# A hybrid decoder step: the last memory update reordered, and four sequences' cached values side by side on TensorE

## What is computed

```
z = rmsnorm(x) @ w_in                       # q, k, v for two groups of 8 heads, an output gate, gates
o_a = dilated sliding-window attention      # heads of group A, three (window, dilation) patterns
h_b = mLSTM matrix memory                   # heads of group B: C, n, m are carried along
x  += concat(rmsnorm(o_a), sigmoid(gate) * rmsnorm(h_b)) @ w_out
x  += conv_glu(rmsnorm(x));  x += sigmoid(rmsnorm(x) @ w_g) * (p @ w_p)
```

## Time and profile before

| | us |
|---|---|
| median of 3 runs | 3385.48 (3385.16 to 3386.03) |
| the profiled execution's own time | 3385.48 |
| its span | 3383.7 |
| TensorE busy | 3175.6 (94%) |
| VectorE busy | 1972.8 (58%) |
| mean granted TensorE clock | 0.97 of full |

### The profile page before, as it was taken

The page is one execution under the profiler, slowest core; times in us unless marked ns, Lnnn a source line. Parts: engine busy times, 40 slices in busy tenths (PEclk is TensorE's granted clock), DMA queues, the critical chain, the costliest instruction groups (busy, mean ns, idle before and its releaser), DMA issues. The chain is left out here.

```text
span 3383.7 us, 49227 instructions
## 1 busy us (share of the span) xinstructions
PE 3175.6 (94%) x19573; PEld 2881.5 (85%) x19573; DVE 1972.8 (58%) x4354; ACT 980.3 (29%) x2029; POOL 624.9 (18%) x564
## 2 busy tenths in 40 slices
PE   7899999888999999998998998996999999999989
PEld 6777677578999999998987776773989999999988
DVE  5666454666555555558556654557575555555573
ACT  4333334533111111114233333444321112111131
POOL 2001111202231122211211110122032122212210
PEclk8999999889999999999999999997999999999999
DMA  5111122621111111110221111327111111111101
GB/s 158 52 47 45 51 71 68 186 79 51 50 51 51 38 51 50 50 38 19 90 59 51 45 45 43 78 77 208 47 63 48 41 44 57 39 50 38 54 19 68
DMA packets 209869, 208.77 MB, mean 62 GB/s; under 512 B 36676, under 2 KB 183044, under 8 KB 207536
## 3 DMA queue, kind: packets, MB, share of 16 engines
q1 hardware_dynamic: 209640, 205.62, 20.4%
HBM read 173.96 MB, written 31.61 MB: 61 GB/s over the span
## 5 line engine op out<-in xcount | busy, mean ns | idle before, releaser
L791 POOL TENSOR_TENSOR wlo<-raw,whi 128x512 fp32r<-128x512 f32 (+3 forms) x488 | 592.5, 1249 | 2214.3 <-ACT whi L1332 2214.3
L832 PE MATMUL ps<-hi,wlo 128*128 128x344 f32 x2880 | 933.4, 324 | 27.0 <-DVE wb L2219 15.5
L833 PE MATMUL ps<-lo,whi 128*128 128x344 f32 x2880 | 926.7, 322 | 0.0
L834 PE MATMUL ps<-hi,whi 128*128 128x344 f32 x2880 | 926.3, 322 | 0.0
L832 PEld LDWEIGHTS ps<-hi,wlo 128*128 128x128 f32 x2880 | 547.4, 190 | 29.9 <-DVE wb L2219 16.1
L833 PEld LDWEIGHTS ps<-lo,whi 128*128 128x128 f32 x2880 | 547.2, 190 | 0.6
L834 PEld LDWEIGHTS ps<-hi,whi 128*128 128x128 f32 x2880 | 547.2, 190 | 0.0
L832 PE MATMUL ps<-whi,lo 128*128 128x512 f32 (+5 forms) x1152 | 448.0, 389 | 19.4 <-ACT zt L1387 18.6
L834 PE MATMUL ps<-whi,hi 128*128 128x512 f32 (+5 forms) x1152 | 425.3, 369 | 0.0
L833 PE MATMUL ps<-wlo,hi 128*128 128x512 f32 (+5 forms) x1152 | 423.6, 368 | 0.0
L2231 DVE TENSOR_TENSOR X<-X,ps 128x344 f32<-128x344 f32 x528 | 268.4, 512 | 196.1 <-PE ps L834 195.6
(11 more groups left out here) (293 smaller groups left out, 3962.6 us busy)
## 6 DMA issues: line engine op xcount, KB each, us to landing
raw<-in_w_up SPq DMA_DIRECT2D x44, 1024.0 KB, 5.1
raw<-in_w_in SPq DMA_DIRECT2D x112, 256.0 KB, 4.6
raw<-in_w_down SPq DMA_DIRECT2D x22, 1024.0 KB, 4.9
kvb<-in_cache_win_k SPq DMA_DIRECT2D x48, 256.0 KB, 3.2
cache<-in_cache_win_v SPq DMA_DIRECT2D x42, 256.0 KB, 5.5
x_scratch<-X SPq DMA_DIRECT2D x8, 1032.0 KB, 5.0
X<-x_scratch SPq DMA_DIRECT2D x4, 2064.0 KB, 14.2
raw<-in_w_out SPq DMA_DIRECT2D x8, 1024.0 KB, 6.4
```

The lines of the kernel that those rows point to most:

```text
L791: pool.tensor_tensor(out=wlo[:, s, r], in0=raw[:, s, r], in1=whi[:, s, r].bitcast(F32), op=ALU.subtract).then_inc(w_split, 1)
L832: nc.tensor.matmul(out, a_lo, b_hi, start=first, stop=False)
L833: nc.tensor.matmul(out, a_hi, b_lo, start=False, stop=False)
L834: return nc.tensor.matmul(out, a_hi, b_hi, start=False, stop=last)
```

## The change

- **The values of four sequences side by side.** `pZ` holds 32 columns for each pattern and sequence instead of a staircase of 64. The 24 products become two groups of 12 (at c = 3 and at c = 5), each of four sequences: sequence g of a group writes PSUM rows 32g to 32g + 31, with a stationary block of 128 x 32, in bank 6 or 7. So the sum that follows runs on 128 rows x 2 banks, and the new token's own part, which was added in place, goes through DRAM: a store (`Sd[2]`), a wait for it, and four loads into `so`. The result goes back by four stores instead of one.
- **Order of VectorE's list.** The root of the attention output's squares moves from the head of the last pair to c = 2, behind `memory_gates`, which comes there from c = 3; `memory_keys`, `memory_output`, `memory_update` come one step earlier each (c = 3, 4, 5). At c = 6 the squares of tiles 0 to 4, their root and `normalise(0)`, `normalise(1)` are done; tiles 5 to 7 follow later.
- **TensorE** turns y tile 0 ahead of the turn of the last memory; **ScalarE** does the output gate behind the exponentials of the decay, and scales and rounds each w_out block in two steps.
- **SyncE.** w_out blocks 2 and 3 come behind `zb` and the slices 0 to 9; `state_C` behind the thirteen small loads; half of x behind the gate's round trip; the own part's store, a wait for it and its four loads come next; then one wait for 12 products, and the slices 19 to 23.

```diff
@@ sp, pair 6 and last pair
-                    load_pair(p + 3)
+                    if p < 2 * PAIRS - 2:
+                        load_pair(p + 3)
...
                 sp.wait_ge(*at(gemm_done, GEMM_OUT))
-                sp.dma_start(lof[:, 0:2048], A["state_C"][l].rearrange("b h (x v) k -> (b h x) (v k)", x=2)).then_inc(cst_in, 16)
...
                     sp.dma_start(zb[:, j, :], Zd[j].rearrange("b (h d) -> (b h) d", d=HD)).then_inc(zb_in, 16)
+                for i in range(10):
+                    load_values(i)
+                load_pair(2 * PAIRS + 1)
...
                 sp.dma_start(mz[:, 2 * HD:2 * HD + 32], Zd[5].rearrange("b (r d) -> (b r) d", d=32)).then_inc(mz_in, 16)
-                for i in range(19):
+                sp.dma_start(lof[:, 0:2048], A["state_C"][l].rearrange("b h (x v) k -> (b h x) (v k)", x=2)).then_inc(cst_in, 16)
+                for i in range(10, 19):
                     load_values(i)
...
                     load_y(t)
-                sp.dma_start(X[:, 0:4, :], Xd[:, 0:4, :]).then_inc(x_back[0], 16)
                 sp.wait_ge(*at(o_exp, PAIRS))
                 sp.dma_start(Zd[6, :, WA - P:WA], zt[0:NB, last % 2, NT, OG:ZW]).then_inc(z_stored[last % 2], 16)
                 sp.wait_ge(*at(z_stored[1], stored_value(last)))
                 sp.dma_start(mz[:, 2 * HD + 32:3 * HD], Zd[6].rearrange("b (r d) -> (b r) d", d=32)).then_inc(mo_in, 16)
+                sp.dma_start(X[:, 0:4, :], Xd[:, 0:4, :]).then_inc(x_back[0], 16)
+                sp.wait_ge(*at(own_done, 1))
+                sp.dma_start(Sd[2].rearrange("b (h d) -> (b h) d", d=HD), sv[:, 0, :]).then_inc(own_stored, 16)
+                sp.wait_ge(*at(own_stored, 16))
+                sp.wait_ge(*at(pz_set, 2))
+                for g in range(4):
+                    sp.dma_start(so[32 * g:32 * g + NH, :, :], Sd[2][g:NB:4, :].rearrange("j (h d) -> h j d", h=NH)).then_inc(so_in, 16)
+                sp.wait_ge(*at(v_used, 12))
                 for i in range(19, 24):
-                    sp.wait_ge(*at(v_used, i - 18))
                     load_values(i)
@@ pe, sample_values
-                        for i in range(5 * c - 15, min(3 * NB, 5 * c - 10)) if c >= 3 else ():
-                            b, r = divmod(i, 3)
-                            a = r * WA + b * HD
-                            pe.wait_ge(*at(v_in[i // 6], 96))
-                            nc.tensor.matmul(ps[0:HD, 6, :], pZ[:, a:a + HD], value_place(i), start=(i == 0), stop=(i == 23)).then_inc(v_used, 1)
+                        if c not in (3, 5):
+                            return
+                        half = (c - 3) // 2
+                        for x in (0, 1):
+                            pe.wait_ge(*at(v_in[2 * half + x], 96))
+                        for r in range(3):
+                            for g in range(4):
+                                b = 4 * half + g
+                                a = (r * NB + b) * 32
+                                nc.tensor.matmul(ps[32 * g:32 * g + 32, 6 + half, :], pZ[:, a:a + 32], value_place(3 * b + r),
+                                                 start=(r == 0), stop=(r == 2)).then_inc(v_used, 1)
...
+                    if q + 1 == PAIRS:
+                        turn_y(0)
                     pe.wait_ge(*at(c_upd, 9 * (q + 1)))
@@ act, last pair
-                    if q + 1 == PAIRS:
-                        output_gates(p)
...
                         do(nc.scalar.activation(sm, sm, ACT.Exp, scale=SCALE, bias=small[:, 10:11], accum_out=small[:, 11:12]), sp_exp)
+                        output_gates(p)
...
-                for t in range(3):
-                    y_high(t)
+                y_high(0)
+                output_squares(PAIRS - 1, NT - 1)
+                y_high(1)
+                y_high(2)
@@ dve, last pair
                         elif c == 2:
                             sample_turned()
+                            memory_gates()
+                            rsqrt(yrs[:, 0:NT], yt2[:, 0:NT], ssq[:, 0:NT], WA, ya_rs)
                         elif c == 3:
-                            memory_gates()
+                            memory_keys()
                         elif c == 4:
-                            memory_keys()
+                            memory_output()
                         elif c == 5:
-                            memory_output()
+                            memory_update()
                         elif c == 6:
-                            memory_update()
+                            y_root(0, 5)
+                            normalise(0)
+                            normalise(1)
...
+                normalise(2)
+                dve.wait_ge(*at(cs_out, 16))
                 for t in range(3):
-                    normalise(t + 2)
...
                     y_low(t)
+                y_root(5, NT)
+                normalise(3)
+                normalise(4)
+                sample_out()
                 sample_sum()
```

More of the change, by code:

```diff
@@ L1055, in gate_columns, with turn_y @@
                     mm.then_inc(gc_ready, 1)
+                def turn_y(t):
+                    m = rows(t)
+                    pe.wait_ge(*at(yn_done, t + 1))
+                    if t < NT:
+                        pe.wait_ge(*at(ya_done, t + 1))
+                    if t >= 2:
+                        n = min(t - 1, NT - 1) + t // NT
+                        pe.wait_ge(*at(yh_done, 2 * n))
+                        pe.wait_ge(*at(yl_done, 2 * n))
+                    for k in range(KT):
+                        mm = nc.tensor.transpose(ps[:, y_bank(t) + k // 4, (k % 4) * m:(k % 4 + 1) * m],
+                                                 y_stage(t)[0:m, k * P:(k + 1) * P], ident[0:m, 0:m])
+                    mm.then_inc(yt_ready, 1)
                 for q in range(PAIRS):
@@ L1187, in turn_embedding @@
                     mm.then_inc(pt_ready, 1)
-                for t in range(3):
+                for t in (1, 2):
                     turn_y(t)
@@ L1949, in memory_update, with y_root, normalise @@
                     do(v.scalar_tensor_tensor(out=Cs, in0=Cs, scalar=iw_, in1=Ct, op0=ALU.mult, op1=ALU.add), mem_done)
+                def y_root(first, end):
+                    dve.wait_ge(*at(ysq_done, NT * (PAIRS - 1) + end))
+                    own = slice(NT + 1 + first, NT + 1 + end)
+                    do(v.tensor_reduce(out=ssq[:, own], in_=ysq[:, :, first:end].rearrange("p q t -> p t q"), axis=AX.X, op=ALU.add))
+                    rsqrt(yrs[:, own], yt2[:, own], ssq[:, own], WA, None)
+                def normalise(t):
+                    m = rows(t)
+                    y = y_stage(t)
+                    rs = yrs[0:m, NT + 1 + t:NT + 2 + t]
+                    if t < NT:
+                        dve.wait_ge(*at(yb_done, NT * (PAIRS - 1) + t + 1))
+                        dve.wait_ge(*at(yst_in[t % 4], 16 * (t // 4 + 1)))
+                        do(v.tensor_scalar(y[:, WA:D - P], y[:, WA:D - P], rs, None, ALU.mult), wait=False)
+                        do(v.tensor_scalar(y[:, D - P:D], yb[:, t, :], rs, None, ALU.mult), yn_done, wait=False)
+                    else:
+                        do(v.tensor_scalar(y[0:m, 0:WA], y[0:m, 0:WA], yrs[0:m, NT:NT + 1], None, ALU.mult), wait=False)
+                        do(v.tensor_scalar(y[0:m, WA:D], y[0:m, WA:D], rs, None, ALU.mult), yn_done, wait=False)
                 for q in range(PAIRS):
@@ L1972, in _ @@
                     evac_k(p)
-                    if last:
-                        rsqrt(yrs[:, 0:NT], yt2[:, 0:NT], ssq[:, 0:NT], WA, ya_rs)
                     if q:
@@ L1992, in queries_scaled @@
                         do(v.tensor_copy(cwb[:, :], iwb[:, P - 1:SEQ:P]))
-                        do(v.tensor_tensor(out=iwb, in0=qT[:, :], in1=iwb, op=ALU.mult), ib_used)
+                        do(v.tensor_tensor(out=iwb, in0=qT[:, :], in1=iwb, op=ALU.mult))
                         if q > 1:
```

98 lines of the change are left out of this document (37 added, 61 removed).

## The result

The kernel after takes 3408.14 us (median, 3403.99 to 3410.15), the kernel before beside it on the same chip 3385.76 us (3385.16 to 3386.11): a ratio of 1.0066, 95% interval 1.0054 to 1.0078. The profiled execution took 3409.46 us and its span is 3407.6 us, 23.9 us more than before.

A forecast was written before the change was run, and what follows sets the result against it. TensorE's dense weight products bound the kernel, so each microsecond the first w_out product moves counts; late value slices move it 7.3 us per layer, + 14.6 us for two: 3385.5 + 14.6 = 3400 us, own range 3391 to 3408 (chance 0.52).

The forecast's parts named there:

- The sign and the mechanism: Slower: in each layer's last pair late value slices (last at 685.5) hold the second group 14.5 us; w_out 7.3 us later.
- one constant: From the second group's start to the first w_out product, through updates, VectorE's steps and turns: 28.3 us.
- The group: TensorE's 12 value products, side by side in column blocks and begun at half clock, take 5.3 us.
- the rival, 13.1 us: Column blocks don't run side by side: a group takes 13.1 us, 7.8 more per layer, kernel 3416; chance 0.10.
- The slow stretch: DMA behind the n_p stores moves 61 GB/s from 635 to 643, now falling on the first value slices.
- The own part's store: SyncE's store of the own part waits behind half of x (2.11 MB, 5.8 us) and lands at 678.3.
- the rival in which it does: The own part's store passes half of x: 5.8 us fall away, kernel 3388; chance 0.22 together with a short hole.
- The step that was too small: SyncE's issues (13 x 0.64 + 19 x 0.50 + 3 us) are done by 657; DMA engines are through at about 669.
- Layer 1: Same order and nearly the same times as layer 0: 7.3 us later there too, + 14.6 us for both layers.
- The rival "no wait": Last slice is there when TensorE comes at 671.0; w_out at 699.3, 7.2 us earlier, kernel 3371; chance 0.16.

The follow-up runs named there:

- x behind: The kernel after, with half of x loaded behind value slices 19 to 23: 3394.45 us, ratio to the kernel before 1.0030.
- own store early: The kernel after, with the own value's store issued right behind the last small load, x left in place: 3400.62 us, ratio to the kernel before 1.0049.
- n_p late: The kernel after, with the third memory pair's n_p stores issued behind slices 19 to 23: 3403.79 us, ratio to the kernel before 1.0057.
- w_out early: The kernel after, with w_out's blocks 2 and 3 loaded in their old place: 3397.07 us, ratio to the kernel before 1.0034.
- all three: The kernel after, with w_out in its old place, n_p stores and half of x behind slices 19 to 23: 3381.10 us, ratio to the kernel before 0.9991.
- the old queue: All the change's work, with SyncE's list in the order of the kernel before plus the own store and its return: 3389.52 us, ratio 1.0016.
- the old work with the early queue: The kernel before, with SyncE's list of the 3368 run (slices early, n_p stored late): 3378.27 us, ratio to the kernel before 0.9981.
- the last slices early: The kernel after, n_p late, w_out early, slices 0 to 11 first, 19 to 23 ahead of every return trip: 3368.14 us, ratio 0.9951; the fastest run.
- in the early queue: The 3368 run with the third pair's n_p stores put back ahead of the sample loads: 3372.84 us, ratio to the kernel before 0.9968.

## Why the prediction was right, and the step that was too small

*The sign and the mechanism held.* The last slices set the end of the stretch: TensorE idles 13.07 us ahead of the second group (14.5 predicted), released by the value cache's DMA. That the two waits agree so well is luck in part, for both of its ends came later than predicted: the slices were there at 689.4 and not 685.5, and TensorE came to them at 676.4 and not 671.0, since the first group had waited for its own slices until 665.2 and not 660.5. The median, 3408.14, lies at the very end of the forecast's own range, 3391 to 3408. The kernels with the new work whose second group waits for slices give one constant from its start to w_out in layer 0: 28.5 us after, and 28.1, 28.8, 28.6, 29.0, 28.6 and 28.5 in the runs with x behind, own store early, n_p late, w_out early, all three and the old queue (28.3 predicted).

*The group.* 5.25 us at half clock (5.3 predicted). The price of the rival, 13.1 us, was measured as well: 13.12. At half clock the old product's 0.90 us would be 1.80 (an estimate); 5.25 us for twelve are 0.44 each, a quarter. The Trainium skill, TensorEngine Tiling (Array Packing), "Theoretical Speedup", gives a speedup of up to 4 for 32 columns; the trace agrees.

*The slow stretch* lay where predicted, 633 to 642 at 41 GB/s, full rate from 642.

*The own part's store* needed 7.9 us behind half of x (7.8 predicted, 670.5 to 678.3). It did not pass it; the rival in which it does is out. The Trainium skill, DMA: Bandwidth & Descriptors, "Queues, rings and completion order", says that each DMA engine takes its work in ring order and that a later transfer may complete first. The runs agree with the first half: where the own store stands right behind half of x it takes 7.0 to 7.9 us, and in the old order the gate's store behind half of x takes over 12. No run here shows the second half.

*The step that was too small* is "Issuing isn't the limit: ... done by 657". It took each issue at its undisturbed price, and it priced the thirteen small loads at 1.1 us of transfer, although they hold SyncE for 8.3 us in which nothing large is issued. The slices' ten took 9.81 us and not 5, w_out's 2.08, the first small load 3.62, so that state_C went out at 657.3 and slice 18 at 662.7, y's three by 664.9; the DMA engines stood nearly still from 654 to 658 in between. Against 362 GB/s, the 105 and 12 GB/s of those 4 us lack some 3.4 us of transfer (an estimate), nearly all of what is missing here: the gate's store is back at 673.3 instead of 669.5, and this 3.8 us runs through unchanged. Last slice at 689.4 and not 685.5, w_out at 717.95 and not 713.8.

Two edits move the gate store: w_out's load out of the way by 7.6 us (1.9 of them because the stretch starts earlier), the n_p stores out of the way by 6.4 (658.62; 2.1 of them the same). They don't tell issuing from transfer: the 5.7 us left for w_out are what the prediction gave its transfer, 5.8. But the run with w_out early has the dry stretch without the blocked issue, so the small loads one by one are enough for it.

*Layer 1* was taken as equal, + 7.3; w_out's shift there, beyond that of layer 0, is + 13.0. But the stretch itself loses hardly more or less than in layer 0. Counted from the y store at its head, w_out comes 11.5 us later than before in layer 0 and 11.1 in layer 1. The other 1.9 us arise between the two stretches: layer 1's already begins 13.3 us late.

```profile
2291.93 0.38 SPq L670 DMA_DIRECT2D y_scratch<-yb  x1
```

```profile
2305.21 0.39 SPq L676 DMA_DIRECT2D y_scratch<-yb  x1
```

They arise in the first attention pairs of layer 1, and the granted clock (PEclk, third number from the end) shows with what. Before, and after:

```profile
1660.00:1820.00 160.00, 148.62 (x919) 134.04 (x919) 100.82 (x234) 60.91 (x136) 30.21 (x31) 0.99 0.20 57
```

```profile
1672.00:1832.00 160.00, 148.58 (x889) 134.40 (x887) 99.42 (x232) 58.79 (x133) 28.73 (x30) 0.97 0.20 57
```

Half of the full clock is granted for some microseconds more there (0.91 on average from 1792 to 1812, where before it was 1.00 from 1780 to 1800). The 0.97 and a later begin stand together in the other kernels as well: 0.99 in the runs with w_out early and the old work with the early queue, where layer 1's stretch begins 1584.3 and 1585.6 us behind layer 0's w_out (1585.4 before), and 0.97 in those with the old queue, all three edits and the last slices early, with 1586.8 to 1587.3. Why the clock is lower there no run shows; the change leaves TensorE's list as it was in that part.

In sum, 14.6 us were predicted; w_out moved by 24.4 in the profiled execution, which took 1.3 us more than the median, and the medians differ by 22.4. Of the 9.8 us missing at w_out, 4.1 lie in layer 0's stretch (3.8 of them by the late gate store) and 3.8 in layer 1's, whose small loads dry the engines out in the same way (30 GB/s from 2329 to 2332); 1.9 lie between the two.

*The rival "no wait"* was priced at 3371 and could not come about with this queue. Once the queue was mended the run gave 3368, but that is not the rival's own path. In layer 0 the second group started at 665.0 and not 671.0, and from there to w_out it was 32.3 us and not 28.3, since VectorE was still busy with the steps ahead. The two differences partly cancel in w_out's 697.3 (699.3 predicted).

## What to carry over

A list of DMA issues is a list of waits as well as of bytes: put what somebody waits for ahead of the bulk, and never a small store whose return the issuing engine awaits right behind 2 MB that nobody needs yet. When a change groups work so that it needs all of its data at once, first find the last piece's issue and what the issuing engine waits for ahead of it. If a good change of the work measures slower, try it with the old order and the old work with the new order before dropping it; here the two halves cost 5 and 10 us, and with a third order the same work gained 16, of which that order brought 6 on the old work too.

## What was not expected of the hardware

An issue is not a fixed price. The same 256 KB load took SyncE 0.50 us with the queue flowing and 0.98 in the slow stretch, and the first issue behind ten slices and two w_out blocks 3.38 to 4.22 us (in the kernel after and the runs that keep that order), though it is only a 16 KB load. With no w_out blocks ahead of it, it took 0.66.

Two stores of 64 elements of 4 bytes each (n_p) are followed by a slow stretch of all transfers behind them: 41 to 80 GB/s for 7 to 9 us. It was 281 GB/s with the stores moved away, and in the early queue 48 for 5 us with them back. The DMA share in it is 0.76 to 0.87: the engines count as busy and move little.

VectorE's smallest operations became seven times as long while GpSimd ran its splits. In the kernel after, VectorE's timeline and GpSimd's:

```profile
661.77 0.17 DVE L1711 SCALAR_TENSOR_TENSOR yrs<-yt,yrs 128x8 f32<-128x8 f32 x1
661.97 1.12 DVE L1708 SCALAR_TENSOR_TENSOR yt<-yrs 128x8 f32<-128x8 f32 x1
663.12 1.19 DVE L1709 SCALAR_TENSOR_TENSOR yt<-ssq,yt 128x8 f32<-128x8 f32 x1
```

```profile
661.78 4.95 POOL L808 TENSOR_TENSOR wlo<-raw,whi 128x512 fp32r<-128x512 f32 x4 [12.78 <-ACT whi L1358]
```

0.17 us become 1.12 to 1.19, from the moment at which GpSimd starts, and the slow operations start about 1.2 us apart, while the four of GpSimd take 1.24 each: as the rows look, one of VectorE gets through per one of GpSimd. The slowing moves with GpSimd's splits (at 654.5 in the fastest run, 658.6 with the old queue), and the kernel before has it too, but no run moved the splits alone. Here it lies under a wait. In the fastest version VectorE is what TensorE waits for, and these four operations take some 4 us more than undisturbed (an estimate); keeping them apart from the splits would be the next thing to try, and that wasn't done.
